# Last norm of a decoder step: the three-term residual sum taken from VectorE and ScalarE and made by TensorE in PSUM

## What is computed

```python
def _layer_out(h, mix, w_out, ln1_g, ln1_b, w_gr, b_gr, w_er, b_er, w_g, w_u, w_d, ln2_g, ln2_b):
    x = _layer_norm(ALPHA * h + mix @ w_out, ln1_g, ln1_b)
    return _layer_norm(ALPHA * x + _hier_moe(x, w_gr, b_gr, w_er, b_er, w_g, w_u, w_d), ln2_g, ln2_b)
```

## Time and profile before

| | us |
|---|---|
| runs timed | 3740.99, 3745.70, 3749.00 |
| median | 3745.7 |
| the profiled execution, its own time | 3730.53 |
| its span, first to last instruction | 3728.5 |
| mean granted clock of TensorE | 0.907 |

### The profile page before, as it was taken

One profiled execution on the slowest core, in us unless ns is written; L12 is line 12 of the kernel. 1 busy time (PEld: TensorE's weight loads), 2 busy tenths in 40 slices (PEclk: granted clock), 3 DMA queues, 4 the chain that ended last, 5 costly groups with the idle time before them and its releaser, 6 DMA issues.

```text
span 3728.5 us, 54744 instructions
## 1 busy us (share of the span) xinstructions
PE 3242.1 (87%) x22252; PEld 2008.2 (54%) x22252; DVE 1274.4 (34%) x3192; ACT 912.9 (24%) x1913; POOL 584.4 (16%) x587
## 2 busy tenths in 40 slices
PE   7997888998889979999499878899898999699990
PEld 3445667777666544333244566777767755334330
DVE  4103444444443351111341134444434434411116
ACT  0001233434442101111110113334434321011111
POOL 1000011111100013343300001111111000243333
PEclk9995899999999989999699869899989899799995
DMA  6112122222213229994721211222221132599826
GB/s 251 53 39 64 44 76 76 76 76 73 73 54 114 86 81 404 408 416 174 280 88 39 83 33 62 76 76 76 76 71 51 50 125 78 215 386 414 349 80 225
DMA packets 168757, 519.40 MB, mean 139 GB/s; under 512 B 41472, under 2 KB 82368, under 8 KB 143168
## 3 DMA queue, kind: packets, MB, share of 16 engines
q0 software_dynamic: 65600, 337.74, 23.6%
q1 hardware_dynamic: 83328, 106.86, 9.2%
q10 hardware_dynamic: 19584, 71.31, 4.9%
HBM read 630.21 MB, written 86.89 MB: 192 GB/s over the span
## 4 chain that ended last, share of the span: by engine, by line
PE 75%; DVE 9%; DMA 7%; ACT 4%; issue 2%; DVEq 2%; POOL 0%; ACTq 0%; SPq 0%; POOLq 0%
PE ps L770 65%; PE ps L767 10%; DMA w_slots<-in_w_gu,rowA 4%; DVE grams L2126 2%; DMA c_x<-xd 1%; DVE S_all L2524 1%; ACT PT L1863 1%; DVE PT L2547 1%; DVE c_x L2162 1%; DMA c_b<-ybd,dga 0%; ACT S_all L1832 0%; ACT kT L1591 0%; ACT PT L1591 0%; DMA xb<-xd,idall 0%; DVE t L2126 0%
## 5 line engine op out<-in xcount | busy, mean ns | idle before, releaser
L770 PE MATMUL ps<-w_slots,xbT 128*64 128x512 f32 (+1 forms) x2048 | 468.4, 609 | 27.3 <-DMA w_slots<-in_w_gu,rowA 23.4
L770 PE MATMUL ps<-hT,w_in 128*128 128x512 f32 x896 | 390.6, 597 | 3.2 <-ACT hT L1591 3.2
L770 PEld LDWEIGHTS ps<-w_slots,xbT 128*64 128x64 f32 x2048 | 175.0, 140 | 276.7 <-issue 261.8
L770 PE MATMUL ps<-grams 128*128 128x128 f32 (+1 forms) x2448 | 294.2, 276 | 29.5 <-DVE grams L2126 23.1
L770 PEld LDWEIGHTS ps<-grams 128*128 128x128 f32 (+1 forms) x2448 | 272.1, 188 | 51.0 <-issue 28.0
L770 PEld LDWEIGHTS ps<-hT,w_in 128*128 128x128 f32 x896 | 170.9, 192 | 216.1 <-issue 211.0
L770 PE MATMUL ps<-w_out,o_mixT 128*128 128x512 f32 x576 | 260.9, 600 | 1.3 <-DVE o_h L2745 1.3
L1591 ACT ACTIVATE kT<-ps 128x512 f32<-128x512 f32 x320 | 188.1, 596 | 254.4 <-PE ps L767 252.4
L770 PE MATMUL ps<-w_slots,hidT 128*64 128x512 f32 (+1 forms) x1024 | 233.9, 598 | 1.2 <-ACT hidT L1591 1.2
L2914 DVE SCALAR_TENSOR_TENSOR gt<-gt,ps 128x256 f32<-128x256 f32 x64 | 26.9, 421 | 517.8 <-ACT gt L2071 517.8
L767 PE MATMUL ps<-cst,S_all 128*128 128x128 f32 x832 | 159.9, 311 | 20.3 <-ACT PT L1591 20.3
(11 more groups left out here) (376 smaller groups left out, 5139.8 us busy)
## 6 DMA issues: line engine op xcount, KB each, us to landing
ybd<-yb ACTq DMA_DIRECT2D x64, 512.0 KB, 8.3
pd<-stage SPq DMA_DIRECT2D x56, 256.0 KB, 2.5
out_y<-c_h ACTq DMA_DIRECT2D x27, 512.0 KB, 2.9
w_in<-in_w_in SPq DMA_DIRECT2D x6, 2048.0 KB, 25.4
o_mixT<-mixd SPq DMA_DIRECT2D x18, 512.0 KB, 3.5
o_h<-out_y SPq DMA_DIRECT2D x18, 512.0 KB, 4.7
xd<-o_x ACTq DMA_DIRECT2D x18, 512.0 KB, 2.8
c_x<-xd ACTq DMA_DIRECT2D x18, 512.0 KB, 6.8
```

The costliest lines, as they stand in the source:

```text
L770: return pe.matmul(out, lhsT, rhs, start=start, stop=stop, skip_group_check=True)
```

## The change

For the last norm only, the sum ALPHA * x + g_a * r_a + g_b * r_b is made by TensorE. ACT writes 19 diagonal 128x128 matrices (the identity times ALPHA, and times each tile's two columns of gates) into the bytes of w_in, all ahead of the first store_rows. Then scaled(L, t) is gone. TensorE makes, for each half of 512 columns, three products that add in one PSUM bank; last_sum[t % 4] is a pair of banks. DVE's two additions are gone; variance and the first operation of norm_x read PSUM. The gather of tile t + 3 waits for the sum of tile t in place of "v".

```diff
@@ plan
-                    T["act"].plan(("norm", l, t), ["ax"])
+                    T["act"].plan(("norm", l, t), ["dg"])
+                    T["pe"].plan(("norm", l, t), ["s"])
@@ build
+        def diag(k):
+
+            return flat(w_in)[:, P * k:P * k + P]
+
+        last_sum = [ps[:, 1024 * k:1024 * k + 1024] for k in range(4)]
@@ POOL, gather
-                if t >= 3:
+                if t >= 3 and l == L:
+                    pool.wait_ge(pe_m.sem, pe_m.at(("norm", l, t - 3), "s"))
+                elif t >= 3:
                     pool.wait_ge(dve_m.sem, dve_m.at(("norm", l, t - 3), "v"))
@@ TensorE
+            def last_sums(t):
+
+                pe.wait_ge(act_m.sem, act_m.at(("norm", L, t), "dg"))
+                pe.wait_ge(x_in[t % 3], 16 * (L * 3 + t // 3 + 1))
+                pe.wait_ge(ya_in[t % 3], 32 * (3 * (L - 1) + t // 3 + 1))
+                if t >= 4:
+                    pe.wait_ge(dve_m.sem, dve_m.at(("norm", L, t - 4), "x"))
+                elif t == 0:
+                    pe.wait_ge(act_m.sem, act_m.at(("moe", L - 1), f"dn{NPAIR - 1}"))
+                    pe.wait_ge(dve_m.sem, dve_m.at(("moe", L - 1), f"yb{NPAIR - 1}"))
+                for q in range(2):
+                    c = slice(512 * q, 512 * q + 512)
+                    mm(last_sum[t % 4][:, c], diag(2 * TILES), c_x[t % 3][:, c], True, False)
+                    mm(last_sum[t % 4][:, c], diag(2 * t), c_a[t % 3][:, c], False, False)
+                    m = mm(last_sum[t % 4][:, c], diag(2 * t + 1), c_b[t % 3][:, c], False, True)
+                m.then_inc(pe_m.sem, pe_m.mark(("norm", L, t), "s"))
...
+            for t in range(TILES):
+                last_sums(t)
@@ ACT, end of the program
-            for t in three:
-                scaled(L, t)
+            act.activation(diag(2 * TILES), ident, ACT.Copy, scale=ALPHA)
+            for t in range(TILES):
+                for k in range(2):
+                    m = act.activation(diag(2 * t + k), ident, ACT.Copy, scale=gates[:, k, t:t + 1])
+                m.then_inc(act_m.sem, act_m.mark(("norm", L, t), "dg"))
             for t in range(TILES):
                 store_rows(L, t)
-                if t + 3 < TILES:
-                    scaled(L, t + 3)
@@ DVE, norm_x and norm_v
-                normalized(("norm", l, t), c_x[u], c_h[u], lnr)
+                normalized(("norm", l, t), c_x[u] if l < L else last_sum[t % 4], c_h[u], lnr)
 
             def norm_v(l, t):
                 u = t % 3
+                if l == L:
+                    dve.wait_ge(pe_m.sem, pe_m.at(("norm", l, t), "s"))
+                    variance(("norm", l, t), last_sum[t % 4])
+                    return
```

## The result

| | before | after |
|---|---|---|
| runs timed together | 3740.99, 3745.70, 3749.00, 3734.53 | 3776.47, 3775.57, 3772.82, 3776.24 |
| median | 3743.3 | 3775.9 |
| ratio, after to before | | 1.0063, 95% interval 1.0042 to 1.0085 |
| span of the profiled execution | 3728.5 | 3773.7 |

The changed kernel is slower, by 0.6%. The ratio makes it 23.6 us (15.7 to 31.8); the two medians lie 32.6 us apart. The forecast was +16.2 us, 3762 us, with 3751 to 3772 as its range; the median of 3775.9 lies outside, the ratio times 3745.7 (3769.3) inside. (The ratio isn't that of the medians.) The first question is thus whether the rest, 7 to 16 us, is the change's.

What follows compares the result with a forecast made beforehand. VectorE was taken as near its bound, with a two-tile loop through the load of c_x, 15.85 us a round, setting the pace. Start +5.6, rounds +12.3, end -1.7 make +16.2; 3745.7 + 16.2 = 3762 us, range 3751 to 3772.

Steps and rivals of the forecast that it cites:

- Start: Last norm, first rows to end of norm_x(0): 7.9 + 5.2 + 1.8 + 2.7 us, ending 5.6 us later than before.
- Rounds: Two-tile loop of the last norm: 20.0 us against 15.85, so +4.1 three times, +12.3 us.
- End: After norm_x(6), last tiles of the last norm: 7.9 us against 9.6, so -1.7 us.
- Sum: Last norm in all: 5.6 + 12.3 - 1.7 = +16.2 us, giving 3762 us.
- VectorE's wait for TensorE: Sign to look for in the profile after: near 45 us in all, in place of the wait for ScalarE.
- The edits costed at nothing: Last norm: 19 diagonals on ScalarE, 5.7 us hidden behind gathers; VectorE reading PSUM adds nothing, ±0.1 us a tile for BATCH_NORM_STATS2.
- Full clock throughout: Rival: TensorE keeps full clock in the last norm; +6 us, 3752 us; chance 0.10.
- The clock that never returns: Rival: TensorE stays at half clock in the last norm; +36.6 us, 3782 us; chance 0.08.
- A sum of less than 3.9 us: Rival: a last-norm sum costs less than the 3.90 us it replaces; 3738 us at 2.6 us a sum; chance 0.06.
- The weakest step: Whole kernel: the profiled execution's difference carries over to the median of the runs, 3745.7 + 16.2 = 3762 us.
- the bounds: Around 3762 us: half-clock length -3.4 or +1.7, loads -4 or +1, runs within 8 us; so 3754 to 3769.
- the two couplings: Last norm: norm_x(t) queued behind the wait for sum t + 1, load t + 3 behind norm_x(t); no separate size given.

Runs made afterwards that it cites:

- b_x_first: Changed kernel with VectorE's last-norm order turned to norm_v(t), norm_x(t) for each tile; last stage 79.6 us, ratio to the kernel before 0.9989.
- b_early_both: Changed kernel with load t + 3 issued when sum t is done and gather t + 3 ahead of ln_root(t); last stage 74.1 us, ratio 0.9968.
- b_one_product: Changed kernel with two of the three products of each sum left out, all waits kept; last stage 86.6 us, ratio to the kernel before 1.0004.
- b_before_deep: Kernel before, with own buffers for x of tiles 3 to 8, load t + 3 issued after norm_v(t); last stage 80.7 us, ratio 0.9976.

## Why the prediction was right, and where it was not

Right in sign, place and mechanism, and in the size of what the last stage lost. Two terms of the round were off and cancelled, which is luck, and the absolute time was too low.

- **Start.** Predicted 17.6 us from the first rows to the end of norm_x(0), measured 3702.06 - 3683.90 = 18.2. Half clock lasted 5.9 us, not 4.3.
- **Rounds.** Predicted 20.0 us. The second operation of norm_x(t) ends at 3702.06, 3722.20, 3742.45 and 3762.77 for t = 0, 2, 4 and 6 (VectorE's timeline, start + 1.28): 20.1, 20.2, 20.3 us, before 15.9, 15.4 and 16.1. Two of its terms were off against each other. The loads on the loop took 8.1 to 8.3 us, where I had 7.2 with 7.5 as the upper bound: I took them as before, and the change made them later. The sums of tiles 3, 5 and 7 took 6.9, 7.2 and 7.3 us, where I had 7.9: half clock lasted 3.0 to 3.7 us and not 4.3, and I had rounded 4.3 us up to six records at half clock where 4.3 / 0.855 is five. The line of c_x (issue to landing) of before, then of after:

```profile
DMA to landing us min/median/max: 4.1/6.3/7.4
```

```profile
DMA to landing us min/median/max: 4.9/7.9/8.3
```

- **End.** Predicted -1.7 us. Measured 3770.48 - 3762.77 = 7.7 against 9.6 before: -1.9.
- **Sum.** +16.2 predicted, +17.4 and +16.0 in the last stages of two profiles, 23.6 and 18.4 by the ratios of the two sets of runs. VectorE's wait for TensorE was to be near 45 us and is 46.6 from the first rows on. The edits costed at nothing were at nothing: the 19 diagonals take 5.7 us in a stretch in which TensorE and VectorE wait for the gathers, BATCH_NORM_STATS2 takes 690 ns from PSUM and 685 from SBUF, the first operation of norm_x 1283 and 1284. The 62 cycles more that the Trainium skill's table gives for PSUM ("VectorE: DVE Perf Modes", the section on the TRN2 errata) are not in these rows.
- **Rivals.** Full clock throughout: not in after, but b_x_first and b_early_both come near it, with rests of 2.1 us at most. The clock that never returns: in no run; b_one_product comes nearest, where five of the nine sums run at 0.50 from end to end. A sum of less than 3.9 us: b_one_product shows that it would have been level, but every fp32 call came as two records. The Trainium skill ("TensorE: Matmul & The Clock Gate", the section on 56 ns against 53.3) has a pitch of 215.7 ns; that is a fourth of the 0.86 us that an fp32 call costs here.
- **The weakest step** is the last: "the difference should carry over: 3745.7 + 16.2". The difference did; the absolute time didn't. Medians of the kernel before are 3743.3 us (4 runs), 3751.9 (31 runs) and 3740.8 (35 runs, on another chip). I had allowed 8 us for single runs, read from three, although the profiled execution of the same kernel, 3730.53 us, lies 10.5 below the lowest of them. Nor do the bounds add up to the range: -7.4 and +2.7 us together, and 8 us for the runs, are wider than 3754 to 3769. The four runs of after in the first set happened to lie within 4 us of each other and above six of the eight later ones.
- **What the prediction overlooked** is the remedy. It named the two couplings (norm_x(t) behind the wait for sum t + 1; the load behind norm_x(t) although TensorE had finished with c_x) and priced neither. Each is worth 23 to 25 us of the last stage, more than the whole loss. Neither figure is the wait alone: without the long rests the clock stays too, which is worth 8 us by the rows of after.

## What to carry to other kernels

An engine that is idle is a free place for work only if nobody waits for the answer: the same 108 records cost nothing unread and 17 us as a link of the loop. Before work is moved to another engine, add up the loop through the buffer that is reused. If the loop stays as it is, the new link must be shorter than what leaves, and at the clock which the engine has after the rests that this loop gives it. When a new reader frees a buffer earlier, move the refill and the order of the queues with it; here that turned a loss of 17 us in the last stage into a gain of 12.

## What the runs showed of the hardware that was not expected

GpSimd's root of one column takes 559 ns in the last stage of after and 1556 ns in that of before, and the issue of its gather 968 in place of 1422 ns for c_a; that for c_b is slower, 1189 in place of 946 ns. Groups of GpSimd in the last stage, before, then after:

```profile
L608 POOL TENSOR_TENSOR lnt<-lnt,cst 128x1 f32<-128x1 f32 x9 | 14.0, 1556 | 35.6 <-DVE lnt L2135 35.6
L708 POOL DMA_INDIRECT c_a<-ybd,dga x9 | 12.8, 1422 | 19.5 <-DMA ybd<-yb 17.8 <-issue 1.7
```

```profile
L717 POOL DMA_INDIRECT c_a<-ybd,dga x9 | 8.7, 968 | 19.4 <-DMA ybd<-yb 17.7 <-issue 1.7
...
L615 POOL TENSOR_TENSOR lnt<-lnt,cst 128x1 f32<-128x1 f32 x9 | 5.0, 559 | 63.3 <-DVE lnt L2164 63.3
```

It is 1555 ns in b_before_deep and 557 in b_x_first. Where it took 1.56 us, VectorE was in an operation over 1024 columns with two SBUF inputs (c_x and c_a, or c_x and lnr); in the kernels with the sums the operations beside it read PSUM or there are none. The slower issue of c_b falls beside the second operation of norm_x, from c_h and lnr (at 3701.53 it takes 1.35 us, with VectorE in that operation from 3700.78 to 3702.06). The Trainium skill ("SBUF — State Buffer", the section on who interferes with whom) says that a VectorE operation with two SBUF inputs contends with a GpSimd instruction that reads SBUF, and that the one which comes second is blocked until the first is done; these rows agree, and the prediction had left it out. It wasn't tried by itself.

Gathers thus start about a microsecond earlier against the loads, which may be why the loads land later: both gathers of tile 4 are now issued ahead of load 3 (at 3700.25 and 3701.53 against 3702.47), where before one of them followed it (3669.08 against 3668.33). In b_x_first, where neither of them is ahead of load 3, the loads on the chain took 6.59 and 7.21 us. That fits, but no run changed this alone: it is argued, not shown.
